# Turning the modulation rows of a decoder step into columns: selecting matmuls or transposes and a sum over groups

## The reference

```python
mod = (jax.nn.silu(c) @ w_ada + b_ada).reshape(B, 6, 1, D_MODEL)
sh1, sc1, g1, sh2, sc2, g2 = [mod[:, i] for i in range(6)]
h = x * (1 + sc1) + sh1
...            # h @ w_in, two attention branches, merged by gates
x = _layer_norm(ALPHA * x + g1 * (merged @ w_o), ln1_g, ln1_b)
h2 = x * (1 + sc2) + sh2
up, gt = jnp.split(h2 @ w_up, 2, axis=-1)
f = (jax.nn.silu(gt) * up) @ w_down
x = _layer_norm(ALPHA * x + g2 * f, ln2_g, ln2_b)
```

## Time and profile before

| | |
|---|---|
| three runs, median (lowest to highest) | 534.76 us (532.82 to 535.14) |
| the profiled execution | 531.78 us, span 530.2 us, mean granted TensorE clock 0.997 |
| busy: PE, PEld, DVE, ACT, POOL | 96%, 88%, 55%, 42%, 18% of the span |
| chain that ended last | PE 81%, DMA 6%, DVE 4%, ACT 3%, SyncE's queue 2% |
| DMA | 115.80 MB, mean 218 GB/s over the span |

### The profile page before, as it was taken

One profiled execution on the slowest core, in us unless ns is written; L12 is line 12 of the kernel. 1 busy time (PEld: TensorE's weight loads), 2 busy tenths in 40 slices (PEclk: granted clock), 3 DMA queues, 4 the chain that ended last, 5 costly groups with the idle time before them and its releaser, 6 DMA issues.

```text
span 530.2 us, 10161 instructions
## 1 busy us (share of the span) xinstructions
PE 508.6 (96%) x3980; PEld 464.5 (88%) x3980; DVE 290.8 (55%) x552; ACT 223.6 (42%) x370; POOL 93.0 (18%) x137
## 2 busy tenths in 40 slices
PE   5899899999999999999999799999999999999997
PEld 4678789888779998986898599999999999999996
DVE  0545676756445463455976867553654444366344
ACT  1333433324445544447444464463444443333312
POOL 2000211125900000000432509641011100000000
PEclk9999999999999999999999899999999999999999
DMA  8999996395996720746344707599877755364102
GB/s 277 391 392 390 383 378 238 121 383 192 292 353 216 260 88 1 238 166 219 100 158 142 239 21 237 164 335 317 311 255 253 257 168 175 107 225 163 41 1 89
DMA packets 85437, 115.80 MB, mean 218 GB/s; under 512 B 3785, under 2 KB 67465, under 8 KB 84884
## 3 DMA queue, kind: packets, MB, share of 16 engines
q1 hardware_dynamic: 83572, 102.76, 57.5%
q0 software_dynamic: 1824, 12.47, 6.5%
HBM read 111.94 MB, written 13.57 MB: 237 GB/s over the span
## 4 chain that ended last, share of the span: by engine, by line
PE 81%; DMA 6%; DVE 4%; ACT 3%; SPq 2%; issue 2%; POOL 0%; ACTq 0%; DVEq 0%; POOLq 0%
PE psum L743 22%; PE psum L745 20%; PE psum L744 20%; DMA raw<-in_w_up 3%; PE psum L917 3%; PE psum L764 2%; PE psum L1037 2%; DMA raw<-in_w_in 2%; PE psum L789 2%; PE psum L990 1%; DMA x_tok<-in_x_sample 1%; ACT w_hi L496 1%; PE psum L1023 1%; PE psum L775 1%; PE psum L981 1%
## 5 line engine op out<-in xcount | busy, mean ns | idle before, releaser
L501 DVE TENSOR_TENSOR w_lo<-raw,w_hi 128x1024 fp32r<-128x1024 f32 (+1 forms) x120 | 147.0, 1228 | 153.9 <-ACT w_hi L496 153.7
L743 PE MATMUL psum<-act_hi,w_hi 128*128 128x288 f32 x736 | 222.7, 303 | 6.1 <-DVE act_lo L1840 3.2
L744 PE MATMUL psum<-act_lo,w_hi 128*128 128x288 f32 x736 | 217.7, 296 | 0.0
L745 PE MATMUL psum<-act_hi,w_lo 128*128 128x288 f32 x736 | 217.1, 295 | 0.0
L496 ACT ACTIVATE w_hi<-raw 128x1024 fp32r<-128x1024 f32 (+1 forms) x120 | 124.2, 1040 | 112.0 <-PE psum L745 88.7
L743 PEld LDWEIGHTS psum<-act_hi,w_hi 128*128 128x128 f32 x736 | 138.7, 188 | 19.9 <-issue 15.0
L745 PEld LDWEIGHTS psum<-act_hi,w_lo 128*128 128x128 f32 x736 | 139.1, 189 | 0.0
L744 PEld LDWEIGHTS psum<-act_lo,w_hi 128*128 128x128 f32 x736 | 139.0, 189 | 0.1
L743 PE MATMUL psum<-f_hi,w_hi 128*128 128x288 f32 x176 | 52.4, 298 | 0.6 <-DVE f_t L1877 0.6
L744 PE MATMUL psum<-f_lo,w_hi 128*128 128x288 f32 x176 | 51.9, 295 | 0.0
L745 PE MATMUL psum<-f_hi,w_lo 128*128 128x288 f32 x176 | 51.8, 294 | 0.0
(11 more groups left out here) (212 smaller groups left out, 583.6 us busy)
## 6 DMA issues: line engine op xcount, KB each, us to landing
raw<-in_w_up SPq DMA_DIRECT2D x22, 1024.0 KB, 5.7
ada_s<-in_w_ada SPq DMA_DIRECT2D x20, 1024.0 KB, 10.7
raw<-in_w_in SPq DMA_DIRECT2D x17, 1024.0 KB, 9.6
raw<-in_w_down SPq DMA_DIRECT2D x10, 1024.0 KB, 5.2
out<-in_cache_kv_a POOLq DMA_DIRECT2D x16, 504.0 KB, 7.4
raw<-in_w_ada SPq DMA_DIRECT2D x4, 1024.0 KB, 6.3
raw<-in_w_o SPq DMA_DIRECT2D x4, 1024.0 KB, 5.4
raw<-in_w_in SPq DMA_DIRECT2D x4, 768.0 KB, 11.4
```

The source lines that it names most:

```text
L501: nc.vector.tensor_tensor(part(w_lo, slot4, by_rows), raw_half(rslot, hh, by_rows), part(w_hi, slot4, by_rows).bitcast(F32), ALU.subtract) ...
L743: nc.tensor.matmul(out, hi_l, hi_r, start=start, stop=False, skip_group_check=True)
L744: nc.tensor.matmul(out, hi_l, lo_r, start=False, stop=False, skip_group_check=True)
L745: return nc.tensor.matmul(out, lo_l, hi_r, start=False, stop=stop, skip_group_check=True)
```

## The change

`ada_turn` uses four transposes against the 128 x 128 identity in place of the four selecting matmuls. Each transposes a full 128 x 128 piece, so the four groups now stand side by side, and the bank is written in all its 512 columns (128 per piece) in place of 36. `ada_add` first sums the four groups on VectorE: a `tensor_reduce` reads columns 32 kk + c (c from 0 to 8) of each of the four pieces, adds over kk and writes 4 x 9 numbers into `mod_t`, an SBUF tile that the kernel already has (it is used otherwise at lines 1675 and 1676). A `link` follows, and the addition of the bias reads `mod_t` in place of the bank. This holds for all twelve steps. Nothing else is touched: not the products, the copy into `rowbuf`, the places of the turns, the semaphores or the loads.

```diff
         pe.wait_ge(ada_row, i + 1)
         for hh in range(4):
-            mm = nc.tensor.matmul(psum[:, ADA_BANK[i], 9 * hh:9 * hh + 9], rowbuf[:, i % 2, 128 * hh:128 * hh + 128],
-                                  cst[:, C_ADA:C_ADA + 9], start=True, stop=True, skip_group_check=True)
+            mm = nc.tensor.transpose(psum[:, ADA_BANK[i], 128 * hh:128 * hh + 128], rowbuf[:, i % 2, 128 * hh:128 * hh + 128], ident)
         mm.then_inc(ada_turned, 1)
...
             dve.wait_ge(ada_turned, i + 1)
+            by_group = psum[:, ADA_BANK[i], :].rearrange("p (h k c) -> p h c k", h=4, k=4)[:, :, 0:9, :]
+            link(V.tensor_reduce(mod_t[:, 0:4, :], by_group, mybir.AxisListType.X, ALU.add))
             if i < 4:
                 V.tensor_tensor(mod[:, 0:16, :].rearrange("p (s m) c -> p s m c", s=2)[:, :, 2 * i:2 * i + 2, :],
-                                psum[:, ADA_BANK[i], 0:36].rearrange("p (s m c) -> p s m c", s=2, m=2),
+                                mod_t[:, 0:4, :].rearrange("p (s m) c -> p s m c", s=2),
                                 lnp[:, 0:16].rearrange("p (s m) -> p s m", s=2)[:, :, 2 * i:2 * i + 2].unsqueeze(3)
                                 .broadcast_to([128, 2, 2, 9]), ALU.add).then_inc(ada_mod, 1)
                 return
-            V.tensor_tensor(mod[:, 4 * j:4 * j + 4, :], psum[:, ADA_BANK[i], 0:36].rearrange("p (h c) -> p h c", h=4),
+            V.tensor_tensor(mod[:, 4 * j:4 * j + 4, :], mod_t[:, 0:4, :],
                             lnp[:, 4 * j:4 * j + 4].unsqueeze(2).broadcast_to([128, 4, 9]), ALU.add).then_inc(ada_mod, 1)
```

## The result

| | median (lowest to highest) | runs |
|---|---|---|
| before | 535.15 us (532.70 to 539.86) | 20 |
| after | 531.78 us (530.29 to 538.19) | 20 |
| ratio after / before | 0.9937, 95% interval 0.9915 to 0.9959 | |

The changed kernel is 0.6% faster: 3.4 us between the medians, 2.2 to 4.5 by the interval. The prediction had said 532.7 us, 2.0 less than before, and had given "faster by over 0.5%" a chance of 0.29. Ratios here leave out executions more than 1.5% above the fastest of their kernel; the fit over the clock further down keeps them, and without them its differences move by 0.2 us at most.

What follows compares the result with a forecast made beforehand. TensorE was taken as the bound (81% of the span in the last-ending chain). Savings 1.68 (turns 4 to 7) + 0.26 (turn 9) + 0.09 (turn 10) = 2.03 us took the median from 534.76 to 532.7, range 530.2 to 535.5.

Steps and rivals of the forecast that it cites:

- Turns 4 to 7: Turns from 56 to 98 us: TensorE sets the pace, whole saving kept, 4 x 0.42 = 1.68 us.
- Turns 0 to 3: Turns from 17 to 40 us: saving lost, lengthening only TensorE's 1.77 us wait ahead of turn 4.
- Turn 8: Turn at 107 us: saving lost, since TensorE's wait ahead of turn 9 grows from 1.15 to 1.57 us.
- Turn 10: Turn at 250 us: VectorE sets the pace; 0.42 gained, 0.33 given back to the reduction, 0.09 us kept.
- TensorE's saving: Each turn: 8 passes of 0.81 us become four transposes of 0.39, saving 0.42 us (bounds 0.37 to 0.46).
- VectorE's price: Each ada_add: reduction 0.30 plus link 0.03, so 0.33 us more (0.22 to 0.72); the addition itself nothing.
- the cover: VectorE's idle times behind turns 5 to 8, put at 1.1 to 2.0 us, hide the added 0.33 us.
- Turn 9: Turn at 124 us: 0.42 saved, 0.16 comes back through delayed copies into tok with 0.17 slack, 0.26 us kept.
- Ahead of turn 9: TensorE's wait for rowbuf behind the load issued at 111.74 us: grows by about 0.4 from 1.15 us.
- rival B: Loads after 102.85 us set the pace, gain of turns 4 to 7 lost: 0.35 us saved, 534.4; chance 0.15.
- Rival A: TensorE's clock falls at 56 us and behind the LayerNorm, 1.5 us each: 535.8, slower; chance 0.13.
- S: Theory formed after the result: part of the difference is a higher mean clock by chance or scatter between jobs.

Runs made afterwards that it cites:

- after: The changed kernel; as a trace, a later profile of it from a repeat without edit, median 531.99 us, ratio 0.9941.
- twice_0_to_3: Kernel before with the selecting matmuls of turns 0 to 3 done twice: 538.14 us, ratio 1.0045.
- reduction_only: Kernel before plus VectorE's reduction and link in each ada_add, result unused, selecting matmuls kept: 535.76 us, ratio 0.9979.
- transposes_only: Changed kernel without the reduction; bias added to the first of four groups only, results not the reference's: 532.28 us, ratio 0.9922.
- turns_4_to_11: Kernel before with transposes and reduction in turns 4 to 11 only: 532.66 us, ratio 0.9926.
- turns_4_to_7: Kernel before with transposes and reduction in turns 4 to 7 only: 534.61 us, ratio 0.9973.
- the first profile: First profiled execution of the changed kernel, no further edit, the slowest of its twenty: 538.19 us.
- same_as_after: The changed kernel again, no edit, for a second profile: 532.23 us, ratio 0.9888.
- turns_0_to_3: Kernel before with transposes and reduction in turns 0 to 3 only: 534.92 us, ratio 0.9972.
- twice_4_to_7: Kernel before with the selecting matmuls of turns 4 to 7 done twice: 541.59 us, ratio 1.0119.
- turns_8_to_11: Kernel before with transposes and reduction in turns 8 to 11 only: 533.90 us, ratio 0.9991.

## Why the prediction was right or wrong

**Which turns count: right, by and large.** Turns 4 to 7 hand their whole saving to turn 8's start (-1.84 us in the trace). Turns 0 to 3 give nothing that can be measured (-0.3 ± 0.7), and the wait ahead of turn 4 takes up part of added work (twice_0_to_3). Turn 8 alone lengthens the wait ahead of turn 9. Turn 10 keeps 0.10.

**TensorE's saving: a term mis-sized.** The prediction took 0.097 us a transpose from six of them and got 0.39 for four; the four take 0.35. It had named this case (a fixed part in the 0.58 us) as its upper bound and chosen the middle. Over turns 4 to 7 this is 4 x 0.04 = 0.16 us more.

**VectorE's price: right**, 0.33 us with the link, but for the addition of the bias at turn 10, which the prediction cost at nothing (within 0.05). Before, it was

```profile
257.13 0.18 DVE L1550 TENSOR_TENSOR mod<-psum,lnp 128x36 f32<-128x36 f32 x1
```

In after it is 0.46 us long there (the line at 256.21 above) and 0.20 at the other turns; the same 0.46 stands in all five profiles in which turn 10 has transposes and the reduction. GpSimd was at work until 256.62 us beside it, and until 256.13, before the addition began, in the kernel before. Whether that is the cause no run settles, and ScalarE's lateness covers it. Behind turn 8 the cover was read wrong: VectorE's first idle time there is 4.03 us, ahead of 122.48, and not one between 1.1 and 2.0.

**Turn 9: a step that failed.** The prediction let 0.16 of 0.42 us come back, because the copies into `tok` start later and TensorE needs their banks two steps later. Almost nothing came back: turn 9 to the keys is 0.47 us shorter (behind a wait a turn takes 0.41 us, where it took 0.91 before), and reduction_only, which has only the delay, is 0.03 longer there. The slack of 0.17 us, read between the end of a copy and the next use of its bank, was too small a reading of the room; the profile of after shows no wait in its place.

**Turn 10: the right number by the wrong account.** It is not the reduction that eats TensorE's gain: transposes_only keeps only 0.12 us there, because ScalarE waits for GpSimd. That 0.09 was forecast and 0.10 measured is luck.

**Ahead of turn 9: not as expected.** The wait was to grow by about 0.4 us and became shorter by 0.1 to 0.5, because the load came 0.7 to 1.0 us sooner. That load's time is open, as told above. This was the place of which the prediction had said that its main assumption would be wrong if it was ("a TensorE earlier at 102 us is still earlier at 124 us"). In the changed kernel the assumption held: SyncE's issue moved from 102.85 to 100.80 us and turn 9 from 124.23 to 121.25. It held in turns_4_to_11 too, without the quicker load: turn 9 starts 66.51 us behind turn 4, 68.20 before. In the profile of turns_4_to_7 it did not, and the wait rose to 2.48 us. So rival B fell for the changed kernel, but its mechanism exists.

**Rival A, the falling clock.** In after the half-clock stretch behind the LayerNorm did not grow (3.0 us below, 3.3 in the earlier trace rows), and the clock ahead of turn 4 stayed up. Stretches of TensorE in after (length, busy and records, granted clock, DMA share, GB/s), the first of them ahead of turn 4, the second from turn 5 past turn 8, the last two behind the LayerNorm:

```profile
54.30:55.70 1.40, 0.01 (x1) 1.00 1.10 348
...
71.00:108.00 37.00, 37.00 (x282) 1.00 0.73 259
300.90:303.90 3.00, 2.91 (x12) 0.50 1.06 361
303.90:306.00 2.10, 1.64 (x12) 1.00 0.41 135
```

The prediction had said that the wait ahead of turn 4 would grow beyond 1.77 us. It did not in the first profile and in after (1.35 and 1.52). In same_as_after it was 1.91 us, and there the clock did fall. From the trace of same_as_after, turn 4 in the timeline, and then the stretch behind it:

```profile
56.89 1.09 PE L789 MATMUL psum<-cst,rowbuf 128*128 128x128 f32 x4 [1.91 <-ACT rowbuf L1288]
```

```profile
57.00:60.00 3.00, 3.00 (x14) 0.50 1.08 394
```

The price of that fall: turn 5 starts 17.20 us behind turn 4, 15.65 in the other two profiles, so 1.55 us, as rival A had priced it (1.5). Falls at this place are also in the traces of turns_0_to_3 and twice_4_to_7, which have selecting matmuls at turn 4, and at turn 9 in turns_0_to_3, turns_4_to_7 and twice_0_to_3, which have them there. That transposes bring the fall about, as the Trainium skill (TensorE: Matmul & The Clock Gate, Part 4: PE-mode transpose) would let one expect, no run here shows: the falls stand behind idle waits, with transposes and with selecting matmuls alike, and the 37 us with turns 5 to 8 in them, which follow matmuls without a wait, stayed at 1.00.

**The total.** By the terms of the prediction with their measured sizes the sum is 1.84 + 0.47 + 0.10 = 2.4 us, where it had said 2.03; with the 0.7 us at turn 8 to turn 9 it is 3.1. All 38 runs of the changed kernel against 104 of before give 2.65 ± 0.45 us at equal mean clock, which does not tell 2.4 from 3.1. The means differ by 3.5, and the rest, 0.8 ± 0.7 us, goes with a mean clock of 0.9914 in place of 0.9899. So by that fit S stands for about a quarter of the difference. Whether the change has a part in that clock is open: reduction_only, which saves nothing, had 0.9916, transposes_only 0.9924, the four kernels with a part of the turns 0.9888 to 0.9910, and the three with added passes 0.9863 to 0.9871. The time came out in the predicted range, but that range (530.2 to 535.5) held the time of before too, so it is the distances, and not the time, that bear the account out. The load that came sooner was no part of the forecast: that share of the gain is luck. The sign was right. "Within 0.5%" had been the likeliest class, and the ratio is just beyond it, with an interval that reaches to 0.9959.

## What to carry to other kernels

A saving on the busiest engine is worth its full size only up to the next place where that engine waits. Go through the places one by one, and ask in each whether the wait grows by what was saved, as turn 8 did alone. Doing a step two or three times is a good test of the same question, but it is one-sided: added work that fills a wait shows slack, and whether removed work pays as much as added work costs has to be measured by itself. (Here the times of turns_4_to_7 alone leave it open.) Where the time lost is not the time added, look whether the clock moved too. And where equal kernels lie 0.4% apart in one job, a change of this size has to be settled by distances in the trace, not by medians.

## What of the hardware was not expected

The mean granted clock goes with the times of the runs of one kernel: 0.52 us for 0.001, so 0.981 to 0.997 spans 8 us in runs of the same program, more than twice what the change brought.

The length of a wait alone does not say whether the clock falls behind it. At turn 4 it was 0.50 behind waits of 1.90 (turns_0_to_3) and 1.91 us (same_as_after) and 1.00 behind 1.77 (before, and the stretch below); at turn 9 it was 0.50 behind 2.48 (turns_4_to_7) and 1.66 (turns_0_to_3) and 1.00 behind 1.82 us (turns_8_to_11). It also fell behind two of the shorter waits. (The stretch in the earlier trace rows from which the prediction read 1.00 ends where turn 4 begins; the one from 56 us on shows it.) Before from turn 4 on, then turn 4 in twice_4_to_7 with a stretch behind it, then turn 9 in twice_0_to_3 with a stretch behind it:

```profile
56.00:60.00 4.00, 3.97 (x31) 1.00 1.10 412
```

```profile
57.28 2.07 PE L789 MATMUL psum<-cst,rowbuf 128*128 128x9 f32 x16 [1.00 <-ACT rowbuf L1289]
...
59.00:60.00 1.00, 1.00 (x6) 0.50 1.16 457
```

```profile
126.36 1.19 PE L789 MATMUL psum<-cst,rowbuf 128*128 128x9 f32 x8 [1.19 <-ACT rowbuf L1289]
...
128.00:129.00 1.00, 1.00 (x6) 0.50 0.39 133
```

The fp32 transposes of a full 128 x 128 block cost 0.35 us for four between other matmuls (0.41 where TensorE had waited ahead of them, 121.25 to 121.66 us in after), against 0.81 (0.91 behind a wait, 124.23 to 125.14 us before) for the eight passes that the four selecting matmuls need, though those write only 9 columns each.
